# Fourteen places of a hand-written order moved where the mixing half of an encoder layer hands over to its feed-forward half

## What is computed

```
mix_out = jnp.einsum('bse,ed->bsd', mixed, w_out[l])
x = _layer_norm(ALPHA * x + (1 + g1) * mix_out) * ln1_g[l] + ln1_b[l]

h = _layer_norm(x) * (1 + sc2) + sh2
a = jax.nn.silu(jnp.einsum('bsd,df->bsf', h, w_gate[l])) * jnp.einsum('bsd,df->bsf', h, w_up[l])
ffn = jnp.einsum('bsf,fd->bsd', a, w_down[l])
x = _layer_norm(ALPHA * x + (1 + g2) * ffn) * ln2_g[l] + ln2_b[l]
```

## Time and profile before

| | |
|---|---|
| median of 3 timed runs | 3006.9 us (3003.96 to 3011.45) |
| profiled execution | 3006.65 us, span 3004.9 us |
| mean granted TensorE clock over the span | 0.986 |
| PE busy | 2899.5 us, 96% |
| DVE, ACT, POOL busy | 71%, 42%, 46% |

### The profile page before, as it was taken

The page is one execution under the profiler, slowest core; times in us unless marked ns, Lnnn a source line. Parts: engine busy times, 40 slices in busy tenths (PEclk is TensorE's granted clock), DMA queues, the critical chain, the costliest instruction groups (busy, mean ns, idle before and its releaser), DMA issues.

```text
span 3004.9 us, 39371 instructions
## 1 busy us (share of the span) xinstructions
PE 2899.5 (96%) x14244; PEld 2437.7 (81%) x14244; DVE 2144.5 (71%) x3092; ACT 1275.0 (42%) x2287; POOL 1393.0 (46%) x1100
## 2 busy tenths in 40 slices
PE   7999998999999998999899999999999999999997
PEld 3888886666666656888799999989999989999996
DVE  5666665988888865566766666667777666777768
ACT  3111112777777765456633323343333233333334
POOL 0233321011111125568745545576677466676754
PEclk9999999999999998999999999999999999999998
DMA  7344347121312106366532122242332233223213
GB/s 262 122 137 133 117 131 187 34 70 57 83 57 71 50 22 207 125 214 210 202 113 71 57 85 71 84 160 77 118 113 78 91 104 139 105 90 114 99 60 116
DMA packets 194061, 333.02 MB, mean 111 GB/s; under 512 B 15366, under 2 KB 102599, under 8 KB 193866
## 3 DMA queue, kind: packets, MB, share of 16 engines
q1 hardware_dynamic: 193868, 330.49, 33.8%
HBM read 250.72 MB, written 79.71 MB: 110 GB/s over the span
## 4 chain that ended last, share of the span: by engine, by line
PE 50%; DVE 4%; POOL 3%; DVEq 1%; ACT 1%; DMA 1%; issue 1%; POOLq 1%; SPq 0%; ACTq 0%
PE tail_bank L2348 9%; PE tail_bank L2350 9%; PE tail_bank L2349 9%; PE tail_bank L2377 5%; PE tail_bank L2378 5%; PE tail_bank L2379 5%; POOL tail_rounded L2077 2%; PE tail_bank L2279 1%; PE tail_bank L2281 1%; PE tail_bank L2280 1%; POOL tail_rounded L2093 1%; DMA tail_plain<-scr_h_d 0%; PE tail_bank L2228 0%; PE tail_bank L2220 0%; POOL tail_plain L2073 0%
## 5 line engine op out<-in xcount | busy, mean ns | idle before, releaser
L2077 POOL TENSOR_TENSOR tail_rounded<-tail_plain,tail_rounded 128x512 fp32r<-128x512 f32 x462 | 656.6, 1442 | 488.5 <-ACT tail_rounded L1844 488.2
L2348 PE MATMUL tail_bank<-tail_rounded 128*128 128x384 f32 x1848 | 622.1, 337 | 19.0 <-DVE tail_plain L2542 10.5
L2350 PE MATMUL tail_bank<-tail_rounded 128*128 128x384 f32 x1848 | 620.8, 336 | 0.0
L2349 PE MATMUL tail_bank<-tail_rounded 128*128 128x384 f32 x1848 | 620.6, 336 | 0.0
L2542 DVE TENSOR_TENSOR tail_plain<-tail_plain,tail_bank 128x384 f32<-128x384 f32 x462 | 247.6, 548 | 262.3 <-PE tail_bank L2350 192.4
L1844 ACT ACTIVATE tail_rounded<-tail_plain 128x512 fp32r<-128x512 f32 x462 | 271.6, 622 | 374.7 <-DVE tail_plain L2518 179.9
L2348 PEld LDWEIGHTS tail_bank<-tail_rounded 128*128 128x128 f32 x1848 | 349.1, 189 | 23.6 <-issue 22.4
L2349 PEld LDWEIGHTS tail_bank<-tail_rounded 128*128 128x128 f32 x1848 | 349.2, 189 | 1.3
L2350 PEld LDWEIGHTS tail_bank<-tail_rounded 128*128 128x128 f32 x1848 | 349.0, 189 | 0.0
L1154 DVE TENSOR_REDUCE att_peak<-att_sc 128x1 f32<-128x1024 f32 x256 | 312.7, 1222 | 41.8 <-PE att_sc L966 35.5
L2377 PE MATMUL tail_bank<-tail_rounded 128*128 128x512 f32 x792 | 310.4, 392 | 11.9 <-DVE tail_plain L2641 4.8
(11 more groups left out here) (290 smaller groups left out, 5132.0 us busy)
## 6 DMA issues: line engine op xcount, KB each, us to landing
tail_plain<-in_w_gu SPq DMA_DIRECT2D x132, 512.0 KB, 4.8
keep_ahead<-in_w_dn SPq DMA_DIRECT2D x66, 512.0 KB, 6.5
proj_ada<-in_w_ada SPq DMA_DIRECT2D x16, 1024.0 KB, 6.8
held_w_hi<-scr_qs_d SPq DMA_DIRECT2D x128, 128.0 KB, 2.9
scr_h_d<-tail_plain SPq DMA_DIRECT2D x63, 256.0 KB, 4.5
proj_x_in<-in_x SPq DMA_DIRECT2D x18, 512.0 KB, 6.5
scr_att_d<-held_w_hi SPq DMA_DIRECT2D x36, 256.0 KB, 2.8
tail_plain<-in_x SPq DMA_DIRECT2D x18, 512.0 KB, 4.2
```

Of the source, the lines that this page charges most:

```text
L2077: nc.gpsimd.tensor_tensor(w_lo[:, j, :], operand(F, j), w_hi[:, j, :].bitcast(F32), ALU.subtract).then_inc(wlo_done, 1)
L2348: nc.tensor.matmul(dst, w_hi[:, j, cols], h_hi[j][:, k, :], start=(k == 0), stop=False)
L2349: nc.tensor.matmul(dst, w_hi[:, j, cols], h_lo[j][:, k, :], start=False, stop=False)
L2350: m = nc.tensor.matmul(dst, w_lo[:, j, cols], h_hi[j][:, k, :], start=False, stop=(k == 3))
```

## The change

No instruction is added or removed; the same work stands in another order, and the chunks of block 0 trade places.

- **SP:** chunks 4 to 11 go to `early`, 12 and 13 to `spare`. So chunks 4 to 7 are asked for right behind the weights of phase 1, 8 to 11 next, and chunks 12 and 13 last. `store_x1(16)` moves behind two stores of the hidden tiles.
- **DVE:** `operands(12)` goes from before the low pieces of chunks 5 to 11 to behind those of chunk 20, in the first gate phase. `residual1(17)` goes ahead of the low piece of chunk 11. `scale_and_shift` of tile 16 moves from ahead of `take_c11` of F = 0 to behind `take_c12`; that of tile 17 from F = 0 to behind `take_v` of F = 1; `operands(14)` goes ahead of the last two `multiply`.
- **ACT:** `moments1` and `normalise1` of tile 16 move from the weights of F = 1 to those of F = 2, behind `copy_first(1)`; those of tile 17 go to G = 1, behind `modulate(16)`. `modulate(15)` moves one place back.
- **POOL:** `rstd1(17)` goes behind the last hidden pieces; `rstd2(16)` and `rstd2(17)` later.
- **PE:** `turn(15)` from F = 0, j = 6 to F = 1, j = 3; `turn(16)` from F = 1, j = 4 to behind all of F = 1.

```diff
@@ h_in @@
-            if b == 0 and i >= 6:
-                return early[:, i - 6, :].bitcast(F32)
+            if b == 0 and i >= 12:
+                return spare[:, i - 12, :]
             if b == 0 and i >= 4:
-                return spare[:, i - 4, :]
+                return early[:, i - 4, :].bitcast(F32)
@@ hidden @@
                 elif c == 4 and b == 0:
+                    sp.wait_ge(mixed, GROUPS * 5)
+                elif c == 12 and b == 0:
                     sp.wait_ge(mlo_done, NT)
-                elif c == 6 and b == 0:
-                    sp.wait_ge(mixed, GROUPS * 5)
@@ sync: loop over r @@
                 if r == 16:
-                    for c in (9, 10, 11, 12, 13, 4, 5):
+                    for c in range(8, 12):
...
                     weights(1)
-                    for c in (6, 7, 8):
+                    for c in range(4, 8):
...
-            for c in range(14, CHUNKS7):
+            for c in range(12, CHUNKS7):
@@ scalar: step @@
                 if G == 1:
                     modulate(NT - 2)
+                    moments1(NT - 1)
                     split_down(0, 0)
+                    normalise1(NT - 1)
...
-                        if G == 0 and j == 3:
-                            moments1(NT - 2)
-                        if G == 0 and j == 4:
+                        if G == 0 and j == 5:
                             modulate(NT - 3)
-                    if G == 0:
-                        normalise1(NT - 2)
...
-                    if G == 0 and j == 4:
-                        moments1(NT - 1)
-                    if G == 0 and j == 6:
-                        normalise1(NT - 1)
+                    if G == 0 and j == 1:
+                        moments1(NT - 2)
+                    if G == 0 and j == 3:
+                        normalise1(NT - 2)
@@ tensor @@
-                    if F == 0 and j == 6:
+                    if F == 1 and j == 3:
                         turn(NT - 3)
-                    if F == 1 and j == 4:
-                        turn(NT - 2)
...
                 phase(b, part, 2 * G + 1)
+                if G == 0:
+                    turn(NT - 2)
@@ vector @@
-            operands(NT - 6)
-            for j in (1, 2, 3):
-                split_h(0, j)
+            split_h(0, 1)
+            split_h(0, 2)
             residual1(NT - 1)
+            split_h(0, 3)
             split_h(0, 4)
...
                     split_h(b, 6)
+                if G == 0:
+                    operands(NT - 6)
...
-                if G == 0:
-                    scale_and_shift(NT - 2)
...
                 take_v(F + 1, up)
+                if G == 0:
+                    scale_and_shift(NT - 1)
...
-                multiply(G, 2)
+                if G:
+                    multiply(G, 2)
                 take_c12(F + 1, up)
-                multiply(G, 3)
                 if G == 0:
                     operands(NT - 4)
+                    multiply(G, 2)
+                multiply(G, 3)
```

More of the change, by code:

```diff
@@ L1697, in _ @@
             weights(2)
-            store_x1(NT - 2)
             store_h2(NT - 4)
             store_h2(NT - 3)
+            store_x1(NT - 2)
             weights(3)
@@ L2136, in _ @@
                     scale_and_shift(t)
-            for j in (1, 2, 3, 4):
+            for j in range(1, OPERANDS):
                 split_h(0, j)
             rstd1(NT - 1)
-            split_h(0, 5)
-            split_h(0, 6)
             def step(b, part, G):
@@ L2147, in step @@
                     shift(io[:, 1, :]).then_inc(y_done, 1)
+                if G == 1:
+                    rstd2(NT - 1)
                 for j in range(OPERANDS):
                     split_w(F + 1, j)
-                    if G == 0 and j == 5:
-                        rstd2(NT - 2)
                 if norms_late(b, part):
@@ L2180, in step @@
                             split_a(G, j - 3)
-                        if G == 0 and j == 4:
-                            rstd2(NT - 1)
+                        if G == 0 and j == 0:
+                            rstd2(NT - 2)
             parts(step)
@@ L2745, in step @@
                 if G == 0:
-                    scale_and_shift(NT - 1)
+                    normalise1(NT - 1)
                 if is_last(b, part):
@@ L2756, in step @@
                     last_sum_w(F + 1)
+                if G == 0:
+                    scale_and_shift(NT - 2)
                 if part and not is_last(b, part):
```

## The result

The changed kernel takes 3013.6 us (median of 13 runs, 3010.84 to 3018.31); the kernel before, timed beside it, 3007.4 us (13 runs). The ratio is 1.0024 with a 95% interval of 1.0017 to 1.0031: 7.2 us slower by the ratio (5.1 to 9.3; the medians lie 6.2 apart), under the 0.3% that the prediction called "same". Predicted were 3011 us, and 3.9 us more than before. The measured time is within the range of 3003 to 3018, and 7.2 is within the "2 to 8 us later" of the forecast, but 3.9 itself lies under the interval.

A forecast was written before the change was run, and what follows sets the result against it. Only the 84 us from the first feed-forward matmul to phase 3 could change, since PE is fully busy behind them. Gains and losses along the path put the third down product 3.9 us later: 3006.9 + 3.9, say 3011 us, range 3003 to 3018.

The forecast's parts named there:

- same: Whole kernel: a change under about 0.3%, 9 us; covers no change and 2 to 8 us later, chance 0.80 together.
- Chunk 4: Operand 1 of F = 0: chunk 4 lands earlier, so it starts at 1442.3 instead of 1444.50, 2.2 us won.
- The residual in the way: Operand 3 of F = 0: DVE's piece of chunk 11 comes behind residual1(17); PE waits 2.8 to 4.2 us, 4.2 taken.
- The sums behind the pieces: Start of F = 1: modulate(14) waits for DVE's later sums; F = 1 starts at 1464.4, not 1467.42, 3.0 us won.
- The turn of tile 15 in F = 1: Operand 4 of F = 1 starts at 1475.75 behind a 2.2 us wait, instead of 1479.24: 3.5 us won.
- The turn of tile 16: Behind F = 1: PE waits 4.5 us for normalise1(16); F = 2 starts at 1487.3, not 1485.6, a loss of 1.7.
- Tile 17: Before the down products: later normalising makes turn(17) wait 4.0 us; third down product at 1513.5, not 1509.63.
- The signs of being wrong: Tile 17's transposes before 1503, or half clock over operands at 1487 to 1496 and F = 2's operand 4 after 1500.
- the first part of the prediction: First feed-forward matmul to phase 3: 21.3 of 84.0 us lost, 13.3 in long waits, most of the other 8 by clock.
- C: Rival, whole kernel: waits move but their total stays, nothing changes in sum, 3006.9 us; chance 0.25.
- B: Rival, feed-forward stretch: early gains kept if tiles 16 and 17 are normalised in time; -8.1 us, 2999 or 2997; chance 0.07.
- A: Rival, clock: half-rate stretches behind the three long waits, two not hidden; +11.9 us, 3019 us; chance 0.13.

The follow-up runs named there:

- e4: Kernel before with only the chunk places and load order of the change; 3010.4 us, ratio 1.0005 to the kernel before.
- e3: Changed kernel with the four sums of tile 12 back ahead of DVE's low pieces; 3014.5 us, ratio 1.0016 to the kernel before.
- e2: Changed kernel with matmuls of no use keeping PE busy in its five longest waits; 3012.4 us, ratio 1.0015 to the kernel before.
- e5: Changed kernel with the normalising of tile 16 on ACT directly behind its moments; 3016.4 us, ratio 1.0024 to the kernel before.
- e11: Changed kernel with e1, e3 and e5 together and DVE's weight sums of F = 2 ahead of scale_and_shift(17); 3004.3 us, ratio 0.9996.
- e12: e11 with the scale and shift of tile 17 directly behind that of tile 16; 3005.9 us, ratio 0.9994 to the kernel before.
- e1: Changed kernel with tile 17's work and the sums of tile 14 back in their places of before; 3008.9 us, ratio 1.0003.
- e6: Kernel before with matmuls of no use keeping PE busy in three of its waits; 3006.8 us, ratio 0.9998 to the kernel before.

## Why the prediction was right, point by point

**Chunk 4: right.** Operand 1 started 2.50 us into the stretch (predicted 2.9, before 5.10). The reason was incomplete: the step credits the chunk's place alone, and e4, with that place and nothing else, has the operand at 5.61. The sums had to leave DVE's way too, as they did in this change.

**The residual in the way: right.** Predicted a wait of 4.2 before operand 3, measured 4.08.

**The sums behind the pieces: the time right, the reason wrong.** F = 1 starts 25.07 us in (predicted 25.0, before 28.02). But e3, with the sums where they stood before, starts it at 24.73. "Taking `scale_and_shift(16)` out of DVE's way to bank 0 is what wins it", says the prediction; e3 agrees with that much (this move was not tried alone), and shows that the sums' move is no part of it. That the start came out at 25.07 is partly luck: a wait of 3.62 us for the sums stands where e3 has none.

**The turn of tile 15 in F = 1: the step that was mis-sized.** Predicted 36.35 for operand 4 of F = 1, measured 38.44. The step "in my sum the half-rate stretches are hidden: behind each stands another wait" left out the wait before F = 1 itself, for which the prediction gave 1.9 to 4.3 us and no price in clock. It was 3.62, the clock fell, and behind it came no wait to take it up, only the path over the turn and `modulate(15)`. The price is 1.55 (e2) to 1.57 us (e5), not the 4 that I gave for one stretch that is not hidden. The wait of 2.31 behind it takes up nothing (2.30 in e5, at full clock). The half clock was shorter here. Windows over one half-rate stretch each, two in the kernel before and this one in the changed kernel:

```profile
1445.00:1454.00 9.00, 8.21 (x32) 0.62 0.68 254
1466.00:1474.00 8.00, 6.58 (x23) 0.57 0.36 142
```

```profile
1469.00:1474.00 5.00, 4.35 (x16) 0.66 0.90 272
```

By these the clock was at 0.50 for about 6.9 us each before, worth 3.4 us of PE at full rate, and for 3.4 us here, worth 1.7. The other 0.5 us are steps that I counted at nothing or too low: about 0.2 from the transposes to ACT behind them (1477.59 to 1478.66, and I had 0.79 for the transposes), 0.14 from the end of the bank copy to PE, and 0.14 over three operands at full clock (6.38 in e2, not 6.24). Together that is the whole miss on the stretch: it is 1.9 too long.

**The turn of tile 16: right as a loss, and the piece to 0.04.** I had a wait of 4.5; it was 2.23, because PE was late itself: by the 2.1 us above, and at half clock for a second time. Either way F = 2's operand 4 waits for `copy_first(2)` and not for PE. e5 takes the wait away and changes nothing at that mark. What the middle piece costs (21.9 against 19.0) is work on DVE and ACT. The prediction had both on this path, "`scale_and_shift(17)` 2.8" and the normalising of tile 16; with most else put back 21.3 remains (e11), and e12 shows 1.1 us of that to be the passes of tile 17 on DVE; the other 1.2 are put down to tile 16 on ACT by argument.

**Tile 17: right, and the largest term.** Predicted 15.9 for the last piece, measured 15.69, before 11.43. The sums of tile 14 beside POOL took from 1495.28 to 1501.10 in the changed kernel, 5.8 (predicted 5.7). e1 undoes this block and gets the 4.3 us of the last piece back, 3.5 in all.

**The signs of being wrong.** Counted from the start of the stretch, the prediction would be wrong if the transposes of tile 17 started before 63.6 (they start at 68.4), or if half clock covered operands between 47.6 and 56.6 and operand 4 of F = 2 started after 60.6. The clock did stand at 0.50 there, for some 3 us, and the operand started at 60.33: the second sign failed to come by 0.3 us.

**The waits cannot be added up**, and here the reading of the first part of the prediction fell: it had 21.3 us lost and 8 of these to the clock. PE's windows there give 6.8, half of the 13.7 us at half clock; e6 gave back three quarters of these and found 1.1. The middle piece is the same to 0.05 us in five profiles with the change's order there, whatever PE did in it (21.88 to 21.93: the changed kernel twice, e2, e3, e5), and to 0.02 in four with the order of before (18.96 to 18.98). A chain over DVE, ACT and POOL sets it, and PE's idle time inside it is only where it shows. What starts the chain is another matter: `copy_first(1)` in the changed kernel, and PE's own operand 4 of F = 1 in the kernel before, so that there PE's lateness at that mark goes through to the end. The last piece is no such constant: 11.43 to 12.72 in the same four profiles, by the clock behind its first wait.

**Rivals.** C (nothing in sum) fell, by the interval of the ratio. B (the early gains kept) needed tiles 16 and 17 normalised in time; e11 does that, and still gives most of the gain back in the middle piece; e12, the best of this kind, wins 2.2 us of the stretch, where B had 8. A named the right mechanism in the wrong place, and at well above its real price. Of the 7.2 us timed (5.1 to 9.3), the stretch explains 4.4 to 5.8. The upper figure is within the interval and the lower just under it, and no profile shows a place for the rest.

## What to carry to other kernels

In a chain of several engines, mark the places where PE waits for the same kind of step each time, and compare the distances between the marks: a distance that stays the same while PE's idle time inside it changes (here to 0.05 us) is set by other engines, and shows what an edit does where the sum of idle times does not. Check at each mark, in each kernel, that PE really waits there: in the kernel before it did not, and its own lost time went through. A piece of work moved away from a wait must be followed to the place where it is done now: here work on two tiles left a phase in which DVE and ACT had idle time and landed on the chain that decides the next two marks. And a wait is priced by what stands behind it: half clock costs nothing ahead of another wait that is long enough, and shows nearly in full (1.55 of 1.7 us) where PE's own work leads to the next mark.

## What the runs showed of the hardware

**The length of a wait alone does not tell whether the clock falls.** It stayed at 1.00 behind waits of 2.96 us (e5), 3.25 (kernel before, first profile) and 3.67 (changed, before the transposes of tile 17), and fell behind 3.05 (e1), 3.25 (kernel before, second profile), 3.62 and even 2.31 (changed), and 3.69 (changed, second profile, before the same transposes). Windows of 2 us behind that last pair, first and second profile:

```profile
1513.00:1515.00 2.00, 1.99 (x14) 1.00 0.04 8
```

```profile
1515.00:1517.00 2.00, 2.00 (x8) 0.50 0.03 8
```

The Trainium skill, page "TensorE: Matmul & The Clock Gate", section "What's actually happening", says that the clock gate goes by how busy the array "has been recently": "the default state is throttled, and activity releases the throttle". That two waits of one length end differently does not go against it; which of the two comes, no run here shows how to foresee.

**DVE and POOL side by side.** Where POOL works too, low pieces took 5.13 us for three on DVE in e3, 1.71 a pair, against 1.58 in the earlier trace rows. The Trainium skill, page "SBUF — State Buffer", section "SBUF: two separate sides", would have 1.85 (an estimate from its rule and the single durations). The runs are all below it: 1.71 is about halfway between the 1.6 that I took and the page's value.
